# Forget rows moved into the query and key tiles, and one up unit of the next group placed ahead of each down product

## What is computed

```
q = rmsnorm_2(q, q_gain); k = rmsnorm_2(k, k_gain)
cum_f = cumsum(log_sigmoid(f_logit + b_f))                # one number for each head and token
s = q @ k^T * 64**-0.5 + cum_f[query] - cum_f[key]        # causal
out = softmax(s) @ v
```

```
u = causal_dwconv(rmsnorm_2(x, g_ffn) @ w_up, ffn_conv_w)
u_gate, u_val = split(u, 2)
x = x + (silu(u_gate) * u_val) @ w_down
```

## Time and profile before

| | us |
|---|---|
| median of 3 runs | 2534.33 |
| lowest, highest | 2530.89, 2536.02 |
| the profiled execution | 2536.04 |
| its span, from first to last instruction | 2534.0 |
| mean granted TensorE clock, as a share of full speed | 0.961 |
| forgetting attention, first logits to last values | 1413.65 to 1524.46 |
| groups of the feed-forward part, first wait to last | 2159 to 2430 |

### The profile page before, as it was taken

The page is one execution under the profiler, slowest core; times in us unless marked ns, Lnnn a source line. Parts: engine busy times, 40 slices in busy tenths (PEclk is TensorE's granted clock), DMA queues, the critical chain, the costliest instruction groups (busy, mean ns, idle before and its releaser), DMA issues.

```text
span 2534.0 us, 26290 instructions
## 1 busy us (share of the span) xinstructions
PE 2367.1 (93%) x10928; PEld 1900.5 (75%) x10928; DVE 1137.1 (45%) x1777; ACT 872.9 (34%) x1346; POOL 345.7 (14%) x303
## 2 busy tenths in 40 slices
PE   7778999999988999999998788999999999899998
PEld 6446888888866568888887647888878788777777
DVE  4873533434224535334444354555233346364553
ACT  4644322223214633222242235453322334142342
POOL 1301200112100002001130001333001111010021
PEclk8799999999988999999999879999999999999999
DMA  3202223333241012333254105224344332232321
GB/s 118 100 1 83 94 89 100 100 100 104 88 149 38 1 50 83 100 100 100 85 90 58 9 1 64 57 47 72 70 75 96 95 100 83 83 100 84 87 87 68
DMA packets 218883, 197.06 MB, mean 78 GB/s; under 512 B 5216, under 2 KB 211500, under 8 KB 218637
## 3 DMA queue, kind: packets, MB, share of 16 engines
q1 hardware_dynamic: 216748, 189.70, 28.1%
q0 software_dynamic: 1504, 5.51, 0.6%
q10 hardware_dynamic: 513, 0.17, 0.0%
HBM read 190.65 MB, written 4.72 MB: 77 GB/s over the span
## 4 chain that ended last, share of the span: by engine, by line
PE 75%; DVE 12%; ACT 7%; issue 2%; DMA 2%; POOL 1%; SPq 0%; POOLq 0%; ACTq 0%; DVEq 0%
PE bank L513 20%; PE bank L515 20%; PE bank L514 20%; PE bank L2072 4%; PE bank L2258 2%; DVE ffn_room L2740 2%; ACT weight_hi L490 2%; ACT nsa_room L804 1%; DVE weight_lo L499 1%; PE bank L687 1%; PE bank L1956 1%; PE bank L840 1%; DVE nsa_room L792 1%; PE bank L1958 1%; DVE dsa_latents L1153 1%
## 5 line engine op out<-in xcount | busy, mean ns | idle before, releaser
L513 PE MATMUL bank<-h_hi,weight_hi 128*128 128x512 f32 (+1 forms) x1576 | 623.5, 396 | 22.2 <-DVE weight_lo L499 16.1
L514 PE MATMUL bank<-h_lo,weight_hi 128*128 128x512 f32 (+1 forms) x1576 | 618.4, 392 | 0.0
L515 PE MATMUL bank<-h_hi,weight_lo 128*128 128x512 f32 (+1 forms) x1576 | 618.2, 392 | 0.0
L499 DVE TENSOR_TENSOR weight_lo<-weight_raw,weight_hi 128x2048 fp32r<-128x2048 f32 (+2 forms) x183 | 387.1, 2116 | 405.7 <-ACT weight_hi L490 405.7
L490 ACT ACTIVATE weight_hi<-weight_raw 128x2048 fp32r<-128x2048 f32 (+2 forms) x183 | 321.4, 1756 | 394.0 <-PE bank L515 350.3
L513 PEld LDWEIGHTS bank<-h_hi,weight_hi 128*128 128x128 f32 (+1 forms) x1576 | 298.9, 190 | 88.2 <-issue 17.2
L515 PEld LDWEIGHTS bank<-h_hi,weight_lo 128*128 128x128 f32 (+1 forms) x1576 | 298.4, 189 | 63.7
L514 PEld LDWEIGHTS bank<-h_lo,weight_hi 128*128 128x128 f32 (+1 forms) x1576 | 299.1, 190 | 61.9
L513 PE MATMUL bank<-hidden_hi,weight_hi 128*128 128x512 f32 x512 | 201.9, 394 | 0.0
L515 PE MATMUL bank<-hidden_hi,weight_lo 128*128 128x512 f32 x512 | 200.8, 392 | 0.0
L514 PE MATMUL bank<-hidden_lo,weight_hi 128*128 128x512 f32 x512 | 198.8, 388 | 0.0
(11 more groups left out here) (409 smaller groups left out, 3260.7 us busy)
## 6 DMA issues: line engine op xcount, KB each, us to landing
weight_raw<-in_w_down SPq DMA_DIRECT2D x40, 1024.0 KB, 5.0
weight_raw<-in_w_up SPq DMA_DIRECT2D x32, 1024.0 KB, 5.4
weight_raw<-in_w_up SPq DMA_DIRECT2D x44, 512.0 KB, 5.1
weight_raw<-in_w_in SPq DMA_DIRECT2D x20, 1024.0 KB, 8.9
weight_raw<-in_w_in SPq DMA_DIRECT2D x26, 512.0 KB, 6.8
weight_raw<-in_w_kv_shared SPq DMA_DIRECT2D x6, 1024.0 KB, 4.9
weight_raw<-in_w_branch SPq DMA_DIRECT2D x6, 1024.0 KB, 4.9
weight_raw<-in_a_w_o SPq DMA_DIRECT2D x4, 1024.0 KB, 5.1
```

The lines of the kernel that those rows point to most:

```text
L499: dve.e.tensor_tensor(split_flat(v, 1), raw_flat(v), f32(split_flat(v, 0)), ALU.subtract).then_inc(*split.mark(("unit", v)))
L513: pe.e.matmul(o, w[0], x[0], start=start, stop=False)
L514: pe.e.matmul(o, w[0], x[1], start=False, stop=False)
L515: return pe.e.matmul(o, w[1], x[0], start=False, stop=stop)
```

## The change

Three things are done.

1. **Forget rows.** The second product of each logit tile is gone. The unused 64 partitions of a head's q and k tile hold the forget rows instead, and one product over 128 rows makes the tile. The two heads of a tile now need tiles of their own: even heads stay in `fq` and `fk`, and `head_norm` writes odd heads to `odd_q` and `odd_k`, by two instructions of 64 partitions in place of one of 128. A new program on GpSimd, `fox_pool`, copies `fu` and writes the masked `fl` into the free halves, two instructions of 64 x 512 for each head. TensorE waits for that program (`("rows", h)`) and no longer for VectorE's L2002, which is gone. `final_factor` moves to `fd`.
2. **Order of units.** `ffn_ups(s)` gives group 0 the ups 0 to 8, group 1 the ups 9 to 16, and group 2 the ups 17 to 21. So one up of the next group is made before the down of each of the first two groups. `weight_plan` follows. The split of the second up unit of a group stands ahead of the group's loop (`split_upto`, and `round_upto` on ScalarE).
3. **Down tiles.** The first two tiles of each `ffn_down` are made by `unit_by_chunk`, the others tile by tile as before.

```diff
+def ffn_ups(s):
+    first, width = ffn_groups()[s]
+    return range(first + (s > 0), min(first + width + 1, FF2_CHUNKS))
...
-        for c in range(first, first + width):
+        for c in ffn_ups(s):
...
+        odd_q, odd_k = y_sc, step(28 * T, 4, T)
...
             def head_norm(t):
                 dve.wait_ge(*mix.pe.when("fox_spread", t))
-                dve.e.scalar_tensor_tensor(fox_head(t), fox_head(t), column("fox_q_gain_2" if t < 4 else "fox_k_gain_2"),
-                                           banks.of("fox_factor", t), ALU.mult, ALU.mult).then_inc(*mix.dve.mark(("fox_scaled", t)))
+                for rows in (slice(0, 64), slice(64, P)):
+                    dst = fox_head(t) if rows.start == 0 else (odd_q if t < 4 else odd_k)[:, t % 4, :]
+                    dve.e.scalar_tensor_tensor(dst[rows], fox_head(t)[rows], column("fox_q_gain_2" if t < 4 else "fox_k_gain_2")[rows],
+                                               banks.of("fox_factor", t)[rows], ALU.mult, ALU.mult
+                                               ).then_inc(*mix.dve.mark(("fox_scaled", t)))
...
         def fox_tensor(pe):
-            pe.wait_ge(*mix.dve.when("fox_scaled", 7))
...
-                    half = 64 * (h % 2)
-                    pe.wait_ge(*fox.dve.when("row", h))
+                    q, k = (odd_q, odd_k) if h % 2 else (fq, fk)
+                    pe.wait_ge(*fox.pool.when("rows", h))
                     def tile(i, bank):
                         S = (i + 1) * P
-                        pe.e.matmul(bank, fq[half:half + 64, h // 2, i * P:S], fk[half:half + 64, h // 2, 0:S], start=True,
-                                    stop=False)
-                        return pe.e.matmul(bank, fu[half:half + 40, i * P:S], per_head[h % 2][half:half + 40, 0:S], start=False,
-                                           stop=True)
+                        return pe.e.matmul(bank, q[:, h // 2, i * P:S], k[:, h // 2, 0:S], start=True, stop=True)
...
         def fox_vector(dve):
-                    if h > 1:
-                        dve.wait_ge(*fox.pe.when("logits", h - 2, NT - 1))
-                    dve.e.tensor_scalar(per_head[h % 2], fl, const[:, C_FOXSEL + h:C_FOXSEL + h + 1], None, ALU.mult
-                                        ).then_inc(*fox.dve.mark(("row", h)))
...
+        def fox_pool(pool):
+            pool.wait_ge(*mix.dve.when("left"))
+            pool.wait_ge(*mix.dve.when("right"))
+            for h in range(FOX_HEADS):
+                t, rows = h // 2, slice(0, 64) if h % 2 else slice(64, P)
+                q, k = (odd_q, odd_k) if h % 2 else (fq, fk)
+                pool.wait_ge(*mix.dve.when("fox_scaled", t))
+                pool.wait_ge(*(fox.pool.last() if h else mix.pool.when("fox_wide", 7)))
+                pool.e.tensor_copy(q[rows, t, :], fu[rows]).then_inc(*fox.pool.mark())
+                pool.wait_ge(*mix.dve.when("fox_scaled", 4 + t))
+                pool.wait_ge(*fox.pool.last())
+                pool.e.tensor_scalar(k[rows, t, :], fl[rows], const[rows, C_FOXSEL + h:C_FOXSEL + h + 1], None, ALU.mult
+                                     ).then_inc(*fox.pool.mark(("rows", h)))
...
         def ffn_tensor(pe):
-                product(pe, ("ffn_down", s), lambda k: chunk(ffn_hidden[s % 2], k), lambda t: (ffn.dve, ("ffn_down", s, t)),
-                        lambda k: (ffn.dve, ("hidden", first + k)))
+                hidden_chunk = lambda k: chunk(ffn_hidden[s % 2], k)
+                hidden_ready = lambda k: (ffn.dve, ("hidden", first + k))
+                unit_by_chunk(pe, ("ffn_down", s), 0, 0, hidden_chunk, lambda t: (ffn.dve, ("ffn_down", s, t)), hidden_ready)
+                per = unit_shape(unit_at["ffn_down", s, 0])[1] // P
+                for t in range(per, NC):
+                    product_tile(pe, ("ffn_down", s, t), unit_of(("ffn_down", s), t, per), t % per, hidden_chunk,
+                                 (ffn.dve, ("ffn_down", s, t)), None, t % per == per - 1)
...
         def ffn_vector(dve):
-                for c in range(first, first + width):
+                split_upto(dve, unit_at["ffn_up", ffn_ups(s)[0], 0] + 1)
+                for c in ffn_ups(s):
```

More of the change, by code:

```diff
@@ L2458, in dn_pool @@
             pool.wait_ge(*fox.act.when("fox_out", FOX_HEADS - 1))
+            pool.wait_ge(*fox.pool.when("rows", FOX_HEADS - 1))
             for dst, name in ((a_log, "dn_a_log_2"), (dt_bias, "dn_dt_bias_2")):
@@ L2691, in ffn_scalar @@
             for s, (first, width) in enumerate(ffn_groups()):
-                for c in range(first, first + width):
+                round_upto(act, unit_at["ffn_up", ffn_ups(s)[0], 0] + 1)
+                for c in ffn_ups(s):
                     for side in range(2):
@@ L2705, in ffn_scalar @@
                     act.wait_ge(*ffn.pool.when("gated", c))
-                    if s > 1:
-                        act.wait_ge(*tile_full.when("ffn_down", s - 2, NC - 1))
-                    act.e.activation(ffn_hidden[s % 2][0][:, c - first, :], conv_bufs[(2 * c + 1) % 6], ACT.Copy
+                    g = c // NC
+                    if g > 1:
+                        act.wait_ge(*tile_full.when("ffn_down", g - 2, NC - 1))
+                    act.e.activation(ffn_hidden[g % 2][0][:, c % NC, :], conv_bufs[(2 * c + 1) % 6], ACT.Copy
                                      ).then_inc(*ffn.act.mark(("hidden", c)))
@@ L2722, in ffn_vector @@
             for s, (first, width) in enumerate(ffn_groups()):
-                for c in range(first, first + width):
+                split_upto(dve, unit_at["ffn_up", ffn_ups(s)[0], 0] + 1)
+                for c in ffn_ups(s):
                     if c == 0:
-                        split_upto(dve, unit_at["ffn_up", c, 0] + 1)
                         vector_stream_factor(dve, ffn, unit_at["ffn_up", 2, 0])
@@ L2734, in ffn_vector @@
                             split_upto(dve, unit_at["ffn_up", c, 0] + 2)
-                        elif c > first:
+                        elif c > ffn_ups(s)[0]:
                             gather(c - 1)
@@ L2897, in pool_program @@
             mix_pool(pool)
+            fox_pool(pool)
             dn_pool(pool)
```

5 lines of the change are left out of this document (2 added, 3 removed).

## The result

The changed kernel took 2461.28 us in the median of four executions (2459.11 to 2463.33), the kernel before on the same chip 2535.18 us (2530.89 to 2539.95). The ratio is 0.9704, with a 95% interval of 0.9692 to 0.9717: 74 us or 3.0% less. The forecast was 2468, so it lies 7 us too high; its own range went from 2460 to 2480, and the result lies 1.3 us inside the low end. The profiled execution of after has a span of 2459.5 us at a mean granted clock of 0.971, against 2534.0 at 0.961 before.

The account below looks back on a forecast made before the run. VectorE's chain and TensorE's logits in series bound the attention; TensorE, with five waits, bounds the feed-forward part. From 2536.0, less 35 and 31.2, came 2469.8, on the median 2468 us; own range 2460 to 2480, with two rivals 2460 to 2489.

Parts of the forecast that it names:

- What bounds the attention: Attention: a head is VectorE's chain plus TensorE's logits, one behind the other, 11.09 us from negation to negation.
- Heads 0 and 1: Attention's opening: VectorE negates head 2 at 1435.8 instead of 1449.66, a gain of 13.9 us.
- Heads 3 to 7: Attention: each head falls to VectorE's chain of 6.95 us, a gain of 26.6 us at full clock.
- one head in five at half clock: Attention: 4.65 us taken off the 40.5 at full clock, on the way to 35 us.
- The shared port: Attention: GpSimd and VectorE locking one another out would make scalings of heads 0 and 1 wait; not shown, no size given.
- The other rule: Attention logits: products in distinct row groups run at once, so the TensorE term would be 0; the prediction saw no overlap.
- The feed-forward part: Feed-forward: waits of 16.8 and 6.1 us go except 0.8, with 9.1 of tails: 31.2 us, bounds 22 and 32.
- the tails: Feed-forward: 47 matmuls at half clock behind the five waits go with them, 47 x 0.193 = 9.1 us.
- the clock stays at half: Rival, attention: TensorE stays at half clock, 17.2 us gained instead of 35, time 2486; chance 0.12.
- the waits change their name: Rival, feed-forward: each of three group heads waits 3.1 us plus a tail, 15 us back, time 2483; chance 0.12.
- the heads don't get shorter: Rival, attention: something else ties logits to VectorE's turn, such as a bank; only 13.9 us comes, 2489; chance 0.05.
- GpSimd becomes the bound: Rival, attention: waits for `rows` make the kernel slower from a pair of 16 us on, 2566 at 20; chance 0.02.

## Why the prediction was right, point by point

**What bounds the attention** was right, and it carried the forecast. The head came out as VectorE's 1.76 + 5.19 = 6.95 us, and the doubled products and the row on VectorE show that it was the coupling: 33.8 of the 41.0 us stay with as many logit instructions as before, and 23 us are lost when the coupling returns with half of them (0.9704 to 0.9794). What the prediction didn't price is that the two causes overlap: removed products are worth 15.9 us with the coupling and 7.2 without.

**Heads 0 and 1**: 13.9 us up to the negation of head 2 were forecast. From the spreads to that negation it was 43.18 us (1406.48 to 1449.66) and is 28.68 (1404.17 to 1432.85), 14.5 less. The half norms cost the upper bound, 0.75 each, as was taken. **Heads 3 to 7**: 26.6 forecast, 61.33 - 34.79 = 26.5 measured. So "together 40.5 at full clock" became 41.0.

**The step that was mis-sized** is the next one: "one head in five at half clock, 4.65 more, and 1 us because VectorE's split ahead of the delta rule is less far ahead". Neither came. The granted clock is 1.00 over the five heads, with idle pieces of TensorE of 0.24 to 0.94 us. The delta rule's first TensorE instruction moved by 43.3 with the negation's 43.4, so no us was lost on the way. This term is 35 against 41.0 and makes 6 of the 7 us by which the forecast is too high.

**GpSimd**: the copy was taken at 0.57 and takes 0.61; the masked row was taken at 1.31 and takes 1.57, inside its bounds. The conclusion, no cost, was right, also at a pair of 3.9 us. The row of 1.31 that was used as a nearest was a different operation, on 128 partitions.

**The shared port** had been left out of the sum for lack of a row. It is shown now: 2.42 us for four scalings beside a busy GpSimd, 1.27 beside an idle one, and the head up to which it lasts moves with the end of GpSimd's program when that is made longer. The Trainium skill, "SBUF — State Buffer" (section "SBUF: two separate sides"), says that GpSimd and certain VectorE instructions exclude one another from a shared port for a whole instruction; by that rule, "scalings of heads 0 and 1 wait", and the trace agrees for head 0. Head 1 escaped because GpSimd had ended.

**The other rule**, of products over few rows in distinct row groups running at once (the Trainium skill, "TensorE: Matmul & The Clock Gate", section "Why this matters for your kernels"), would have made the removed products free. Its condition wasn't met here: the two products of a tile lay on the same partitions. Eight logit instructions take 2.32 us in after and sixteen took 4.52, so no such overlap was there. The prediction's own proof, that 4.52 is twice 2.26, was circular, since 2.26 was half of 4.52; what carried it were the values, 2.42 for the same columns over 128 rows. The stronger form, two products of 64 rows kept on different row groups, wasn't tried.

**The feed-forward part**: 31.2 forecast, 32.3 measured. The waits did what was written: 16.8 to 0.8, 6.1 to nothing, no new wait at a group's head, so 22.1 are waits and 10.2 are what lay behind them. The mis-sized term is the tails, 47 matmuls of 0.193 or 9.1 us; it is 1.1 too small, more than the 0.4 within which this part repeats. About 0.6 of it is the first matmul behind a wait, which in four of the five places took 0.57 to 0.60 to the next start, where the sum took the 0.43 of the others; the rest isn't assigned. The margin of 1.5 us for the first down unit's split held.

**The sum**: 41.0 and 32.3 make 73.3. The 2.3 upstream and the 1.6 given back at the end, of which 1.0 in waits for GpSimd's copies of `xT` (3.2 to 4.2), weren't foreseen and nearly cancel, which is luck. With the 40.5 at full clock, which stood in the text as an end of the range, the forecast would have been 2463.

**The rivals**: "the clock stays at half" (2486) is out by the 1.00; "the waits change their name" (2483) by the missing rows; "the heads don't get shorter" (2489) by the negations 6.95 apart. "GpSimd becomes the bound" is out up to a pair of 3.9 us; a pair of 16 wasn't tried.

## What to carry to other kernels

Look first for an operand that an engine makes late in its turn and that another engine waits for: taking that one instruction off the busy engine was worth more than removing half of the waiting engine's instructions, 33.8 against 15.9 us when each is done alone, and the two together only 41.0. Name the order when you price two changes that shorten the same chain. After that the head's bound is the chain of the engine that was freed, and its waits inside a head are the place to put the work that stands behind them. Two ways of covering the same wait (work of the next group ahead of it, another output tile beside it) don't add up; the second is worth only what the first leaves.

## What the runs showed of the hardware

- VectorE's four `TENSOR_SCALAR` of a head (128x128, 128x256, 128x384 and 128x512 float32, from memory to memory) take 1.27 us with GpSimd idle, and 2.14 to 2.43 with GpSimd running float32 copies and scalings. It isn't a common factor: in head 0 of after they took 0.66, 0.34, 0.83 and 0.82, against 0.29, 0.35, 0.42 and 0.48. A negation of 128x4 took 0.45 to 0.47 there instead of 0.17 (1414.41 and 1421.54 in after), but 0.17 at 1414.83 in the longer GpSimd program. The maxima, which read a PSUM bank, took the same in both cases (0.68 and 0.69 for 128x512).
- TensorE kept its full clock through stretches in which it was busy for 84%, with idle pieces of under 1 us. With waits of 3.4 us in the mean (23.7 in seven) it fell to 0.82 over the same 38 us. Behind the one wait of 3.78 in after's attention the eight instructions of the values took 4.09 us instead of 2.39.
- On VectorE, 64 partitions cost as much as 128: the halves of a norm take 747 ns in the mean, the whole took 0.75 us.
- On GpSimd, a 64x512 float32 product with a column takes 1569 ns and a copy of the same size 608 ns by the profile's lengths, 1.6 and 0.7 from start to start.
- A float32 product over 128 rows takes TensorE as long as one over 64: 2.32 us for the eight instructions of a head, half of the 4.52 for sixteen.
